# Attention by blocks of 256 queries, with one PSUM bank of value sums and two banks for the work placed in between

## The chip, the cores and the metric

The kernel runs on all 8 cores of one Trainium2 chip, each core on half of one of the four sequences. The time is device microseconds of the slowest core. The engines are called PE (TensorE matmul), PEld (its weight load), DVE (VectorE), ACT (ScalarE), POOL (GpSimd) and SP (SyncE).

## The reference, cut to what matters

```python
z = h @ w_in                                   # q, k, v, attention gate, pool input, pool gate
q, k: (B, S, 4 heads, 2, 64);  v: (B, S, 4 heads, 128)
# differential attention, causal, S = 4096
s = einsum('bqhcd,bkhcd->bhcqk', q, k) / 8     # c = 0, 1: two softmaxes of a head
a = softmax(where(causal, s, -inf))
a = a[:, :, 0] - lam * a[:, :, 1]
o = einsum('bhqk,bkhe->bqhe', a, v)
attn_out = rms_norm(o) * (1 - lam_init) * silu(g_attn)
pool_out = multiscale_pool(u) * silu(g_pool)
mix = concat(attn_out, pool_out) @ w_out
h = layer_norm(ALPHA * h + mix)
gate = sigmoid(h @ w_pg + b_pg)
out = h + (p @ w_pe) * gate
```

## The kernel before

Each core holds the keys and values of its whole sequence (8 slabs of 512 positions) and owns 4 groups j = 0 to 3 of 512 queries. All work is written into one stream for each engine in program order, with semaphores between them; an engine never reorders its stream.

The work has stages. Stage A projects the first slabs (no attention). Stage B holds the attention of j = 0 and 1, stage C that of j = 2, stage D that of j = 3. In each of B, C and D a list of other work ("filler") is laid between the pieces of attention: projections of later slabs in B and C; in D the output part, in tiles of 128 tokens: `q_M` (output projection, then the layer norm on DVE and POOL), `q_T` (transpose), `q_G` (gate projection) and `q_P` (embedding projection, product and store). Between the stages stand two blocks of pure projections, `block(5)` and `block(7)`. After D comes the tail, which finishes the tiles that are left.

Attention is a list of 160 steps. A step handles two blocks of 128 keys (u = 0, 1) against the 512 queries of one head. `qk(p)` makes the scores: for each u and softmax c one matmul of 64 rows, 128 keys and 512 queries, each into a PSUM bank of its own (banks 0 to 3); on the diagonal ("stair" steps, 4 for each j and head) the queries shrink to 512, 384, 256, 128 and four matmuls of 128 columns add the mask. ACT takes exp of each pair of banks into `PT[pi]` (L713). `lsum(p)` sums the columns of PT by four matmuls of 32 columns of ones, side by side in the four column tiles of the array, one for each (u, c), into bank 6. `av(p)` multiplies V with PT: four matmuls into banks 4 and 5, one bank for each softmax. The order in the stream is qk(p), lsum(p-1), filler, av(p-1), filler.

At the last step of a head DVE copies the sums to bf16 in two parts (`Lh`, then `Lhl`, L727 and L728) and the value sums to SBUF (`o12`, L744). Then two matmuls `q_sel` (L764) spread the row sums over the partitions, ACT takes Ln and Exp (L768, L770) for the reciprocal, DVE combines the two softmaxes (`fin_o`), squares and splits (`fin_sq`), two matmuls `q_ss` (L783) sum the squares, ACT makes the reciprocal root (L795, L797) and DVE multiplies into `mixT` (`mix`). `after(n, f)` puts f into the stream n calls of `tick()` later.

The filler is dealt out by `Feed`: `take(us)` issues matmuls of the current piece ("quantum", mostly 8 matmuls) until a budget is used or the quantum ends. The filler and the matmuls `q_sel` and `q_ss` all write one PSUM bank, `BF` = 7. So before q_sel or q_ss the quantum in progress is completed (`feed.finish()`), and its result must be read out of the bank (`evac`, L446, L507, L594, L649, L669, mostly on DVE).

```python
feed = Feed([BF])
...
if fq is not None:
    used = feed.take(budget)
    feed.finish()
...
if fq is not None:
    fq.mms[0](BF)
```

In the tail the last four tiles (12 to 15, the tokens of j = 3) go through M, T, G and P.

## Time and profile before

| what | value |
|---|---|
| runs | 829.9, 850.0 and 829.45 us, median 829.9 |
| profiled execution | 823.01 us, span 821.2 us |
| spans of the cores | 813.9 to 821.2 us |
| granted TensorE clock of the cores | 0.964 to 0.970 of full |
| busy of the span: PE, DVE, ACT, POOL | 85%, 45%, 50%, 16% |

The span is from the first to the last instruction of the slowest core; the profiled execution's own time has 1.8 us around it. The profile is that of this slowest core. It has the stages at these times: A 0 to 146.8 us, B to 309.8, block(5) to 325.6, C to 469.4, block(7) to 485.6, D to 743.5, tail to 821.2.

### The profile page before, as it was taken

How to read it: one execution, taken by the hardware profiler on the slowest of the kernel's cores; microseconds unless marked ns; L12 is line 12 of the kernel's file. 1: busy time of each engine (PE TensorE's matmuls, PEld its weight loads, DVE VectorE, ACT ScalarE, POOL GpSimd, SP SyncE). 2: the span in 40 equal slices, each digit the busy share in tenths (PEclk: the TensorE clock that was granted, in tenths of full speed). 3: DMA queues.
4: the chain of work that ended last, by engine and by line, in shares of the span. 5: the costliest groups of instructions: out<-in, count | busy, mean ns of one | idle time of the engine just before them, and what ended most of it. 6: DMA issues, size and time to landing. Idle time of an engine off the chain costs nothing.

```text
span 821.2 us, 9761 instructions; the slowest of 8 cores (813.9 to 821.2 us)
## 1 busy us (share of the span) xinstructions
PE 694.2 (85%) x4122; PEld 275.8 (34%) x4122; DVE 370.6 (45%) x544; ACT 414.3 (50%) x524; POOL 128.2 (16%) x101
## 2 busy tenths in 40 slices
PE   0899999877788989999998987988887987999473
PEld 0344444333233324333333332332332332334231
DVE  1124526354534572423225536444445555547922
ACT  0012112544556675667676644767653756654231
POOL 6000000000000000000000002333331332333322
PEclk9899999999999999999999999999998998999878
DMA  8997330303000000302334080011010141010012
GB/s 99 144 157 108 52 52 1 51 1 52 1 1 1 1 1 1 51 4 49 52 52 78 3 199 31 1 52 51 27 52 27 52 147 58 26 52 27 10 42 103
DMA packets 30187, 40.37 MB, mean 49 GB/s; under 512 B 6336, under 2 KB 25024, under 8 KB 30144
## 3 DMA queue, kind: packets, MB, share of 16 engines
q0 software_dynamic: 24240, 21.24, 18.8%
q1 hardware_dynamic: 5904, 18.52, 6.4%
q8 instruction: 32, 0.52, 0.3%
q14 instruction: 11, 0.09, 0.0%
HBM read 52.60 MB, written 8.39 MB: 74 GB/s over the span
## 4 chain that ended last, share of the span: by engine, by line
PE 60%; DVE 21%; ACT 10%; DMA 4%; issue 2%; POOL 2%; DVEq 0%; ACTq 0%; SPq 0%; POOLq 0%
PE psum_all L462 23%; PE psum_all L738 9%; PE psum_all L700 6%; PE psum_all L579 6%; PE psum_all L635 5%; ACT sb_PT L713 5%; PE psum_all L723 4%; DMA sb_wsec<-w_in 3%; PE psum_all L708 2%; DVE sb_st L597 2%; DVE sb_arena L649 2%; POOL sb_mv L602 1%; DVE sb_Lhl L728 1%; PE psum_all L764 1%; DVE sb_Lh L727 1%
## 5 line engine op out<-in xcount | busy, mean ns | idle before, releaser
L713 ACT ACTIVATE sb_PT<-psum_all 128x1024 bf16<-128x1024 f32 (+3 forms) x320 | 267.1, 891 | 99.2 <-PE psum_all L708 52.5
L462 PE MATMUL psum_all<-sb_xb,sb_wsec 128*128 128x512 bf16 x768 | 189.6, 387 | 19.3 <-DMA sb_wsec<-w_in 19.1
L738 PE MATMUL psum_all<-sb_PT,sb_Vt 128*128 128x512 bf16 (+3 forms) x640 | 146.5, 352 | 0.0
L462 PEld LDWEIGHTS psum_all<-sb_xb,sb_wsec 128*128 128x128 bf16 x768 | 72.1, 99 | 111.0 <-issue 30.6
L700 PE MATMUL psum_all<-sb_qT,sb_kT 64*128 64x512 bf16 (+3 forms) x640 | 94.0, 355 | 14.4 <-ACT sb_PT L713 10.6
L738 PEld LDWEIGHTS psum_all<-sb_PT,sb_Vt 128*128 128x128 bf16 x640 | 60.6, 99 | 61.5 <-issue 3.9
L462 PE MATMUL psum_all<-sb_wsec,sb_xb 128*128 128x512 bf16 x256 | 67.0, 397 | 3.9 <-DMA sb_wsec<-w_in 3.8
L579 PE MATMUL psum_all<-sb_wsec,sb_mixT 128*128 128x512 bf16 x256 | 64.4, 383 | 2.6 <-DVE sb_arena L623 1.8
L723 PE MATMUL psum_all<-sb_PT,sb_ones_bf 128*32 128x512 bf16 (+3 forms) x640 | 59.4, 361 | 0.0
L635 PE MATMUL psum_all<-sb_wsec,sb_arena 128*128 128x512 bf16 x192 | 50.6, 391 | 9.6 <-DVE sb_arena L649 9.4
L154 POOL DMA_DIRECT2D sb_xb<-xT x8 | 7.4, 919 | 307.2 <-PE psum_all L540 140.2
L700 PEld LDWEIGHTS psum_all<-sb_qT,sb_kT 64*128 64x128 bf16 x640 | 21.2, 94 | 82.8 <-ACT sb_PT L713 37.6
L446 DVE CAST sb_Vt<-psum_all 128x512 bf16<-128x512 f32 x22 | 15.1, 688 | 60.4 <-PE psum_all L462 60.4
L653 POOL TENSOR_SCALAR sb_arena<-sb_arena 128x1024 f32<-128x1024 f32 x11 | 31.1, 2832 | 55.9 <-ACT sb_arena L652 55.9
L764 PE MATMUL psum_all<-sb_Lhl,sb_sel 128*128 128x512 bf16 x32 | 12.7, 402 | 28.5 <-DVE sb_Vt L446 7.8
L462 PEld LDWEIGHTS psum_all<-sb_wsec,sb_xb 128*128 128x128 bf16 x256 | 23.7, 101 | 36.2 <-issue 8.3
L446 DVE CAST sb_kT<-psum_all 128x512 bf16<-128x512 f32 x22 | 15.1, 688 | 44.6 <-PE psum_all L462 44.6
L579 PEld LDWEIGHTS psum_all<-sb_wsec,sb_mixT 128*128 128x128 bf16 x256 | 22.4, 98 | 35.1 <-DVE sb_arena L623 6.0
L723 PEld LDWEIGHTS psum_all<-sb_PT,sb_ones_bf 128*32 128x32 bf16 x640 | 16.4, 92 | 45.2 <-issue 38.8
L649 DVE TENSOR_TENSOR sb_arena<-psum_all,sb_wsec 128x512 f32<-128x512 f32 x22 | 15.1, 687 | 36.0 <-PE psum_all L635 36.0
L669 DVE TENSOR_TENSOR sb_arena<-psum_all,sb_arena 128x512 f32<-128x512 f32 x28 | 19.2, 687 | 26.8 <-PE psum_all L663 26.7
L519 DVE TENSOR_TENSOR sb_arena<-sb_arena 128x572 f32<-128x572 f32 (+3 forms) x40 | 29.6, 741 | 1.4
(138 smaller groups left out, 694.9 us busy)
## 6 DMA issues: line engine op xcount, KB each, us to landing
sb_xb<-xT POOLq DMA_DIRECT2D x8, 1024.0 KB, 12.0
sb_wsec<-w_in POOLq DMA_DIRECT2D x5, 1024.0 KB, 45.3
sb_xb<-x_own SPq DMA_DIRECT2D x6, 512.0 KB, 4.9
out<-sb_xb SPq DMA_DIRECT2D x6, 512.0 KB, 2.7
sb_wsec<-w_out POOLq DMA_DIRECT2D x2, 1024.0 KB, 10.4
sb_wsec<-w_pg POOLq DMA_DIRECT2D x2, 1024.0 KB, 11.2
sb_kT<-x_own SPq DMA_DIRECT2D x4, 512.0 KB, 8.4
sb_xh<-x_own SPq DMA_DIRECT2D x3, 512.0 KB, 3.2
```

What stands on the lines that cost most here:

```text
L446: P.op(DVE, lambda e: e.tensor_copy(out=out_ap, in_=src), reads=[B_bank[bank]], writes=wbufs)
L462: P.op(PE, lambda e: e.matmul(ps[:, bank, :], a, b, start=(kc == 0), stop=(kc == 7)), reads=[bw, bx], writes=[B_bank[bank]], sig=(kc == 7))
L519: e.tensor_tensor(out=o, in0=a, in1=b, op=ALU.add), reads=[bs], writes=[bd])
L579: P.op(PE, lambda e: e.matmul(ps[:, bank, :], mixT[:, kc, tsl(t)], wo[nh][:, kc, :], start=(i == 0), stop=(i == 7)), reads=[B_w[1 + nh], B ...
L635: P.op(PE, lambda e: e.matmul(ps[:, bank, :], hb[hs(t)][:, kc * 128:(kc + 1) * 128], wg[nh][:, kc, :], start=(kc == 0 and t < 11), stop=(k ...
L649: P.op(DVE, lambda e: e.tensor_tensor(out=z[:, nh, :], in0=ps[:, bank, :], in1=bpgb[:, nh, :], op=ALU.add), reads=[B_bank[bank], bz], writ ...
L653: P.op(POOL, lambda e: e.tensor_scalar(out=z[:], in0=z[:], scalar1=2.0 ** 62, scalar2=None, op0=ALU.min), reads=[bz], writes=[bz])
L700: P.op(PE, lambda e, c=c, u=u, key0=key0: e.matmul(ps[:, 2 * u + c, q0:512], kT[64 * c:64 * c + 64, h, key0:key0 + 128], qT[j][64 * c:64 * ...
L713: P.op(ACT, lambda e, u=u, pi=pi: e.activation(out=PT[pi][:, :, q0:512], in_=ps[:, 2 * u:2 * u + 2, q0:512], func=AF.Exp), reads=[B_bank[2 ...
L723: P.op(PE, lambda e, c=c, r0=r0, pi=pi: e.matmul(ps[r0:r0 + 32, BL, q0:512], ones_bf[:, 0:32], PT[pi][:, c, q0:512], start=it["first"], st ...
L738: P.op(PE, lambda e, c=c, u=u, pi=pi, s=s, kb=kb: e.matmul(ps[:, BO + c, q0:512], Vt[:, s * 4 + kb, h * 128:(h + 1) * 128], PT[pi][:, c, q ...
L764: P.op(PE, lambda e: e.matmul(ps[:, bank, :], sel[:, c, :], Lhl[:], start=True, stop=True), reads=[B_Lhl, B_sel], writes=[B_bank[bank]])
```

## The change

- The queries are taken by 256. A group is (j, half hf, head h), 32 groups in place of 16. A unit is a pair of key blocks (k = 0, 1) against 256 queries; a step has two units. The scores of softmax c for both key blocks share one bank (2u + c), 256 columns each. There are 144 steps: 2j + 1 in the first half and 2j + 2 in the second, for each head. Only the last step of a group is masked; its units have 256 and 128 queries, and eight mask matmuls.
- Groups of j = 0 and j = 1 alternate in stage B. Stage B has 40 steps, C 44, D 60.
- `PT` is ordered key block, softmax, query, so a moving operand holds both softmaxes (512 columns). `lsum` has a column tile for each (u, key block), bank 5. `av` accumulates both softmaxes side by side in one bank, 4. In the first step of the groups of j = 0, hf = 0, a matmul with zeros opens the narrower column tiles.
- Banks 6 and 7 are both for filler; the matmuls q_sel and q_ss are issued by `Feed.now` into the other bank than that of the quantum in progress, which stays open.
- A group needs one `q_sel` matmul (before: two for a head) and two `q_ss` matmuls of 256 columns. Squaring moves from DVE to ACT, the split squares have buffers of their own (`sqx`), and there are six sets of finishing buffers, not two. Read-outs of filler by `evac` within attention are all on DVE.
- In stage D the first 256 queries of j = 3 are finished for all heads after 28 of 60 steps. The filler of D covers tiles 0 to 13 (M) in place of 0 to 11, G to tile 11, P to tile 10, T to tile 12, and T(0) comes after M(1). The tail finishes tiles 14 and 15, with T(14) and T(15) behind P(12) and P(13).

The diff, cut to its core (of what is removed, most stands in the functions above and is left out here; of the buffers, loads and hooks only the size of PT):

```diff
+    def _next(self):
+        b = self.banks[self.bi % len(self.banks)]
+        self.bi += 1
+        return b
+
     def _open(self):
         if self.cur is None and self.q:
             self.cur, self.k = self.q.popleft(), 0
-            self.bank = self.banks[self.bi % len(self.banks)]
+            self.bank = self._next()
+        return self.cur is not None
+
+    def now(self, q):
+        b = self._next()
+        if self.cur is not None:
             self.bi += 1
-        return self.cur is not None
+        for m in q.mms:
+            m(b)
+        q.end(b)
...
+        BL, BO = 5, 4
...
+        PT = [sb(f"PT{i}", [128, 2, 2, 256], BF16) for i in range(4)]
...
+                    if t + 4 < 14:
                         load_x(t + 4)
             return Quantum([mm(kc) for kc in range(2)], end, 2 * MM)
 
 
+        order = []
+        for hf in range(2):
+            for h in range(4):
+                order += [(0, hf, h), (1, hf, h)]
+        order += [(j, hf, h) for j in (2, 3) for hf in range(2) for h in range(4)]
         steps = []
...
+        for n_, (j, hf, h) in enumerate(order):
+            units = [((s, kb), (s, kb + 1), 0, False) for s in range(2 * j) for kb in (0, 2)]
+            units += [((2 * j, kb), (2 * j + 1, kb), 0, False) for kb in range(2 * hf)]
+            units += [((2 * j, 2 * hf + i), (2 * j + 1, 2 * hf + i), 128 * i, True) for i in range(2)]
+            for i in range(0, len(units), 2):
+                steps.append(dict(j=j, hf=hf, h=h, n=n_, slot=(n_ % 4 if j < 2 else 4 + n_ % 2), u=units[i:i + 2],
+                                  first=(i == 0), last=(i + 2 == len(units))))
         NS = len(steps)
...
         def qk(p):
             it = steps[p]
...
+            j, h, hf = it["j"], it["h"], it["hf"]
+            for u, (a, b, q0, msk) in enumerate(it["u"]):
+                for k, (s, kb) in enumerate((a, b)):
+                    key0 = s * GT + kb * 128
                     for c in range(2):
...
+                        P.op(PE, lambda e, c=c, u=u, k=k, key0=key0, q0=q0, msk=msk: e.matmul(
+                            ps[:, 2 * u + c, 256 * k + q0:256 * k + 256], kT[64 * c:64 * c + 64, h, key0:key0 + 128],
+                            qT[j][64 * c:64 * c + 64, h, 256 * hf + q0:256 * hf + 256], start=(k == 0), stop=(k == 1 and not msk)),
+                            reads=[B_k[h][s], B_q[h][j]], writes=[B_bank[2 * u + c]], sig=(c == 1 and k == 1 and not msk))
+            for u, (a, b, q0, msk) in enumerate(it["u"]):
+                if not msk:
+                    continue
+                for k, (s, kb) in enumerate((a, b)):
+                    mk = 2 if k else kb % 2
+                    for c in range(2):
+                        P.op(PE, lambda e, c=c, u=u, k=k, mk=mk, q0=q0: e.matmul(
+                            ps[:, 2 * u + c, 256 * k + q0:256 * k + q0 + 128], ident[:], tri3[:, mk, :], start=False, stop=(k == 1)),
+                            writes=[B_bank[2 * u + c]], sig=(c == 1 and k == 1), deps=t_id)
+            for u, (a, b, q0, msk) in enumerate(it["u"]):
                 pi = 2 * (p % 2) + u
...
+                P.op(ACT, lambda e, u=u, pi=pi, q0=q0: e.activation(
+                    out=PT[pi][:, :, :, q0:256].rearrange("p k c n -> p c k n"),
+                    in_=ps[:, 2 * u:2 * u + 2, :].rearrange("p c (k n) -> p c k n", k=2)[:, :, :, q0:256], func=AF.Exp),
+                    reads=[B_bank[2 * u], B_bank[2 * u + 1]], writes=[B_PT[pi]])
...
         def lsum(p):
             it = steps[p]
...
+            for u, (a, b, q0, msk) in enumerate(it["u"]):
                 pi = 2 * (p % 2) + u
...
+                for k in range(2):
+                    r0 = 32 * (2 * u + k)
+                    wide = it["first"] and q0 > 0
+                    if wide:
+                        P.op(PE, lambda e, k=k, r0=r0: e.matmul(ps[r0:r0 + 32, BL, :], zero[:], PT[2 * (p % 2)][:, k, :, :],
+                                                               start=True, stop=False),
+                             reads=[B_PT[2 * (p % 2)], B_one], writes=[B_bank[BL]], sig=False)
+                    P.op(PE, lambda e, k=k, r0=r0, pi=pi, q0=q0, wide=wide: e.matmul(
+                        ps[r0:r0 + 32, BL, :].rearrange("p (c n) -> p c n", c=2)[:, :, q0:256], ones_bf[:, 0:32], PT[pi][:, k, :, q0:256],
...
         def av(p):
             it = steps[p]
...
+            h = it["h"]
+            for u, (a, b, q0, msk) in enumerate(it["u"]):
                 pi = 2 * (p % 2) + u
...
+                for k, (s, kb) in enumerate((a, b)):
+                    P.op(PE, lambda e, k=k, u=u, pi=pi, s=s, kb=kb, q0=q0: e.matmul(
+                        ps[:, BO, :].rearrange("p (c n) -> p c n", c=2)[:, :, q0:256], Vt[:, s * 4 + kb, h * 128:(h + 1) * 128],
+                        PT[pi][:, k, :, q0:256], start=(it["first"] and u == 0 and k == 0), stop=(it["last"] and u == 1 and k == 1)),
+                        reads=[B_PT[pi], B_v[s * 4 + kb]], writes=[B_bank[BO]], sig=(k == 1))
             if it["last"]:
...
+        def q_sel(it):
+            f_ = it["slot"]
+            o_, r_, x_, bo, br, bx = o12[f_], rr[f_], sqx[f_], B_o12[f_], B_rr[f_], B_sqx[f_]
 
             def fin_o():
...
+                P.op(DVE, lambda e: e.tensor_tensor(out=o_[:], in0=o_[:], in1=r_[:], op=ALU.mult), reads=[bo, br], writes=[bo])
+                P.op(DVE, lambda e: e.scalar_tensor_tensor(out=o_[:, 0, :], in0=o_[:, 1, :], scalar=neglam, in1=o_[:, 0, :],
+                                                           op0=ALU.mult, op1=ALU.add), reads=[bo, B_sc], writes=[bo])
+                P.op(ACT, lambda e: e.activation(out=r_[:, 0, :], in_=o_[:, 0, :], func=AF.Square), reads=[bo], writes=[br])
+
+            def fin_sq():
+                P.op(DVE, lambda e: e.tensor_copy(out=x_[:, 0, :], in_=r_[:, 0, :]), reads=[br], writes=[bx])
+                P.op(DVE, lambda e: e.tensor_tensor(out=x_[:, 1, :], in0=r_[:, 0, :], in1=x_[:, 0, :], op=ALU.subtract),
+                     reads=[br, bx], writes=[bx])
+
+            def mm(bank):
+                P.op(PE, lambda e: e.matmul(ps[:, bank, :], sel[:, 1, :], Lhl[:], start=True, stop=True),
+                     reads=[B_Lhl, B_sel], writes=[B_bank[bank]])
+
+            def end(bank):
+                P.op(ACT, lambda e: e.activation(out=r_[:], in_=ps[:, bank, :].rearrange("p (c n) -> p c n", c=2), func=AF.Ln),
+                     reads=[B_bank[bank], bx], writes=[br])
+                P.op(ACT, lambda e: e.activation(out=r_[:], in_=r_[:], func=AF.Exp, scale=-1.0), reads=[br], writes=[br])
+                after(2, fin_o)
+                after(4, fin_sq)
+            return Quantum([mm], end, MM)
...
+            def mm(i):
+                def f(bank):
+                    P.op(PE, lambda e: e.matmul(ps[:, bank, 0:256], ones_bf[:], x_[:, i, :], start=(i == 0), stop=(i == 1)),
+                         reads=[bx, B_one], writes=[B_bank[bank]], sig=(i == 1))
+                return f
+
+            def mix():
                 P.op(DVE, lambda e: e.tensor_tensor(out=o_[:, 0, :], in0=o_[:, 0, :], in1=r_[:, 0, :], op=ALU.mult),
...
+                     reads=[bo, br], writes=[bo])
                 P.op(DVE, lambda e: e.scalar_tensor_tensor(out=mixT[:, h, tok], in0=o_[:, 0, :], scalar=gsc, in1=mixT[:, h, tok],
                                                            op0=ALU.mult, op1=ALU.mult),
                      reads=[bo, B_sc, B_mix[h][j]], writes=[B_mix[h][j]])
 
```

The filler of stage D, the loop and the tail:

```diff
         fillC += [hook(k7[0], lambda: wload(pTb[:], pT_d.rearrange("(kc p) t -> p kc t", p=128), [B_xb[0]]))] + k7[1:]
         fillC += v7[:3] + [hook(v7[3], load_wout)] + q_q(7) + q_halo(7) + u7[:3] + [hook(u7[3], load_wpg)]
         fillD = []
-        for k in range(12):
+        for k in range(14):
             fillD += [q_M(k, 0), q_M(k, 1)]
-            if k >= 1 and k < 11:
+            if k == 1:
+                fillD += [q_T(0)]
+            if 1 <= k < 13:
                 fillD += [q_G(k - 1, 0), q_G(k - 1, 1)]
-            if k >= 2:
+            if 2 <= k < 13:
                 fillD += [q_P(k - 2, 0), q_P(k - 2, 1)]
-            if k < 11:
+            if 1 <= k < 13:
                 fillD += [q_T(k)]
...
+            budget = feed.left() * weight(p) / sum(weight(i) for i in range(p, end_p))
             tick()
...
+            used = feed.take(budget / 2)
             if p > 0:
                 av(p - 1)
                 if steps[p - 1]["last"]:
...
+                    fins.setdefault(p, []).append(q_sel(steps[p - 1]))
+                    fins.setdefault(p + 3, []).append(q_ss(steps[p - 1]))
             tick()
...
+            for q in fins.pop(p, []):
+                feed.now(q)
+            feed.take(budget - used)
...
+        last = steps[NS - 1]
+        M = {(t, nh): q_M(t, nh) for t in range(14, 16) for nh in range(2)}
+        emit(M[14, 0], 0, 0, 7)
+        emit(M[14, 1], 1, 0, 7)
+        emit(q_sel(last), 6)
+        for p in sorted(fins):
+            for q in fins[p]:
+                emit(q, 7)
+        emit(q_G(12, 0), 5)
+        emit(q_G(12, 1), 6)
+        tail[0] = True
+        emit(q_T(13), 7)
+        emit(M[15, 0], 2, 0, 7)
+        emit(M[15, 1], 3, 0, 7)
         tick()
+        emit(q_P(11, 0), 5)
+        emit(q_P(11, 1), 6)
+        emit(q_ss(last), 7)
         tick()
         tick()
+        emit(q_G(13, 0), 4)
+        emit(q_G(13, 1), 5)
+        for t in (14, 15):
             for nh in range(2):
+                emit(M[t, nh], 2 * (t - 14) + nh, 7)
+        fe = Feed([6, 7, 4, 5, 0, 1, 2, 3])
+        fe.q.extend([q_P(12, 0), q_P(12, 1), q_P(13, 0), q_P(13, 1), q_T(14), q_T(15), q_G(14, 0), q_G(14, 1), q_G(15, 0), q_G(15, 1),
+                     q_P(14, 0), q_P(14, 1), q_P(15, 0), q_P(15, 1)])
```

## Rows read from the trace of the kernel before

**Rows 1.** The page: busy us, share of the span and instructions of each engine

```profile
PE 694.2 (85%) x4122; PEld 275.8 (34%) x4122; DVE 370.6 (45%) x544; ACT 414.3 (50%) x524; POOL 128.2 (16%) x101
```

**Rows 2.** Busy time by stage: us, PE, PEld, DVE, ACT, POOL (xinstructions), clock, DMA share, GB/s

```profile
146.80:309.80 163.00, 136.23 (x933) 53.95 (x933) 82.00 (x120) 95.70 (x132) 0.88 (x1) 0.97 0.09 13
325.60:469.40 143.80, 134.40 (x881) 49.77 (x882) 53.93 (x81) 98.01 (x123) 4.38 (x6) 1.00 0.25 41
485.60:743.50 257.90, 221.93 (x1336) 81.67 (x1337) 134.62 (x179) 157.63 (x182) 80.35 (x54) 0.97 0.15 54
743.50:784.50 41.00, 25.43 (x131) 11.60 (x128) 33.59 (x47) 15.16 (x17) 16.89 (x13) 0.85 0.07 26
784.50:821.20 36.70, 23.11 (x111) 10.15 (x111) 8.43 (x10) 7.63 (x12) 8.01 (x4) 0.83 0.18 72
```

**Rows 3.** Groups of TensorE instructions: shape, count, busy us, mean ns, idle before, releaser

```profile
L635 PE MATMUL psum_all<-sb_wsec,sb_arena 128*128 128x512 bf16 x192 | 50.6, 391 | 9.6 <-DVE sb_arena L649 9.4 <-DVE sb_xh L594 0.2
...
L663 PE MATMUL psum_all<-sb_wsec,sb_xb 128*128 128x512 bf16 x64 | 18.5, 390 | 8.5 <-DVE sb_arena L669 8.1 <-ACT sb_qT L768 0.3
...
L764 PE MATMUL psum_all<-sb_Lhl,sb_sel 128*128 128x512 bf16 x32 | 12.7, 402 | 28.5 <-DVE sb_Vt L446 7.8 <-DVE sb_kT L446 5.2 <-DVE sb_arena L500 4.6
...
L783 PE MATMUL psum_all<-sb_Lh,sb_ones_bf 128*128 128x512 bf16 x16 | 6.2, 388 | 5.6 <-DVE sb_kT L446 2.8 <-DVE sb_Vt L446 1.8 <-DVE sb_arena L649 0.9
```

**Rows 4.** Longest wait of TensorE for exp: us in total, times, longest

```profile
PE psum_all L700 <- ACT sb_PT L713: 10.6, 27, 0.9
```

**Rows 5.** Timeline of TensorE in two diagonal steps: start us, us, instruction

```profile
153.61 0.39 PE L700 MATMUL psum_all<-sb_qT,sb_kT 64*128 64x256 bf16 x4
153.93 0.40 PE L708 MATMUL psum_all<-sb_tri,sb_ident 128*128 128x128 bf16 x4
...
157.69 0.60 PE L700 MATMUL psum_all<-sb_qT,sb_kT 64*128 64x512 bf16 x4
158.22 0.40 PE L708 MATMUL psum_all<-sb_tri,sb_ident 128*128 128x128 bf16 x4
158.55 0.24 PE L723 MATMUL psum_all<-sb_PT,sb_ones_bf 128*32 128x128 bf16 x4
```

**Rows 6.** Timeline of TensorE: a step without filler, then projection matmuls

```profile
299.69 0.40 PE L723 MATMUL psum_all<-sb_PT,sb_ones_bf 128*32 128x512 bf16 x4
300.02 1.04 PE L738 MATMUL psum_all<-sb_PT,sb_Vt 128*128 128x512 bf16 x4
300.99 0.61 PE L700 MATMUL psum_all<-sb_qT,sb_kT 64*128 64x512 bf16 x4
...
309.81 10.52 PE L462 MATMUL psum_all<-sb_xb,sb_wsec 128*128 128x512 bf16 x48
```

**Rows 7.** Timeline of all engines around the end of a head in stage B

```profile
173.40 0.24 PE L723 MATMUL psum_all<-sb_PT,sb_ones_bf 128*32 128x128 bf16 x4
...
174.41 0.75 DVE L728 SCALAR_TENSOR_TENSOR sb_Lhl<-sb_Lh,sb_hl,psum_all 128x512 bf16<-128x512 bf16 x1
```

**Rows 8.** Groups of ScalarE instructions by shape

```profile
L713 ACT ACTIVATE sb_PT<-psum_all 128x1024 bf16<-128x1024 f32 x224 | 215.2, 1019 | 61.5 <-PE psum_all L700 46.1 <-PE psum_all L708 15.0
...
L768 ACT ACTIVATE sb_qT<-psum_all 128x512 f32<-128x512 f32 x18 | 10.6, 595 | 31.6 <-PE psum_all L764 31.6
```

**Rows 9.** Timeline of all engines after the last step of attention

```profile
743.29 0.40 PE L738 MATMUL psum_all<-sb_PT,sb_Vt 128*128 128x128 bf16 x4
...
753.48 3.24 POOL L653 TENSOR_SCALAR sb_arena<-sb_arena 128x1024 f32<-128x1024 f32 x1 [6.35 <-ACT sb_arena L652]
...
758.68 0.69 DVE L594 SCALAR_TENSOR_TENSOR sb_kT<-sb_kT,psum_all 128x512 f32<-128x512 f32 x1 [1.24 <-PE psum_all L579]
...
771.07 1.06 ACT L587 ACTIVATE sb_PT<-sb_kT 128x1024 bf16<-128x1024 f32 x1 [4.37 <-DVE sb_kT L584]
...
784.56 3.59 PE L635 MATMUL psum_all<-sb_wsec,sb_PT 128*128 128x512 bf16 x8 [12.47 <-ACT sb_PT L621]
```

**Rows 10.** Timeline of the last matmuls

```profile
807.81 1.89 PE L663 MATMUL psum_all<-sb_wsec,sb_xb 128*128 128x512 bf16 x8
```

More of the change, by code:

```diff
@@ L566, in build_nc @@
         tail = [False]
+        made = set()
         def load_x(t):
@@ L695, in qk @@
             it = steps[p]
-            j, h, q0 = it["j"], it["h"], it["q0"]
-            for u, (s, kb) in enumerate(it["u"]):
-                key0 = s * GT + kb * 128
-                for c in range(2):
-                    P.op(PE, lambda e, c=c, u=u, key0=key0: e.matmul(
-                        ps[:, 2 * u + c, q0:512], kT[64 * c:64 * c + 64, h, key0:key0 + 128],
-                        qT[j][64 * c:64 * c + 64, h, q0:512], start=True, stop=(not it["stair"])),
-                        reads=[B_k[h][s], B_q[h][j]], writes=[B_bank[2 * u + c]], sig=(c == 1 and not it["stair"]))
@@ L733, in av @@
             it = steps[p]
-            q0, h = it["q0"], it["h"]
-            for u, (s, kb) in enumerate(it["u"]):
+            h = it["h"]
+            for u, (a, b, q0, msk) in enumerate(it["u"]):
                 pi = 2 * (p % 2) + u
-                for c in range(2):
-                    P.op(PE, lambda e, c=c, u=u, pi=pi, s=s, kb=kb: e.matmul(
-                        ps[:, BO + c, q0:512], Vt[:, s * 4 + kb, h * 128:(h + 1) * 128], PT[pi][:, c, q0:512],
-                        start=(it["first"] and u == 0), stop=(it["last"] and u == 1)),
-                        reads=[B_PT[pi], B_v[s * 4 + kb]], writes=[B_bank[BO + c]], sig=(c == 1))
@@ L763, in mm @@
+                P.op(DVE, lambda e: e.tensor_tensor(out=x_[:, 1, :], in0=r_[:, 0, :], in1=x_[:, 0, :], op=ALU.subtract),
+                     reads=[br, bx], writes=[bx])
             def mm(bank):
-                P.op(PE, lambda e: e.matmul(ps[:, bank, :], sel[:, c, :], Lhl[:], start=True, stop=True),
+                P.op(PE, lambda e: e.matmul(ps[:, bank, :], sel[:, 1, :], Lhl[:], start=True, stop=True),
                      reads=[B_Lhl, B_sel], writes=[B_bank[bank]])
             def end(bank):
-                P.op(ACT, lambda e: e.activation(out=r_[:, c, :], in_=ps[:, bank, :], func=AF.Ln), reads=[B_bank[bank]], writes=[br[c]])
@@ L924, in build_nc @@
                 lsum(p - 1)
-            wsum = sum(weight(i) for i in range(p, end_p))
-            budget = feed.left() * weight(p) / wsum
-            fq = fins.pop(p, None)
-            eng[0] = 0
+            budget = feed.left() * weight(p) / sum(weight(i) for i in range(p, end_p))
             tick()
-            if fq is not None:
-                used = feed.take(budget)
-                feed.finish()
-            else:
-                used = feed.take(budget / 2)
+            used = feed.take(budget / 2)
             if p > 0:
```

220 lines of the change are left out of this document (82 added, 138 removed).

## The prediction

> **What bounds the kernel now.** I read the engines' shares first: TensorE is busy 694.2 of 821.2 us, 85%, DVE 45% and ACT 50% [rows 1]. Then the stages. In B, C and D TensorE is busy for 136.2 of 163.0, 134.4 of 143.8 and 221.9 of 257.9 us: it is the bound there, and stands still for 26.8, 9.4 and 36.0 us, 72 together. The tail is another matter: 77.7 us with 48.5 us of TensorE work, and in its first 41 us DVE is busy for 33.6 [rows 2]. So there are three places to look: the work of TensorE in attention, its 72 us of waits, and a tail that DVE bounds.
>
> The waits have a clear owner. L764 (q_sel) sat idle for 28.5 us before its matmuls, L783 (q_ss) for 5.6, the gate and embedding projections L635 and L663 for 9.6 and 8.5, nearly all released by a DVE instruction that reads bank 7 (L446, L500, L649, L669) [rows 3]: 52 us. With the smaller rows of the same kind (L579, 2.6 us, and a transpose that waits for its input, 4 us) I count 59. Waits of the scores for exp are only 10.6 us [rows 4].
>
> **The change part by part.**
>
> *Attention on TensorE.* I need the price of a run of matmuls. From start to start, four score matmuls of 512 columns, run in pairs, take 158.22 - 157.69 = 0.53 us, of 256 columns 0.32 us; four masks of 128 columns one after the other 0.33 us [rows 5]. Four row sums, side by side, take 0.33 us, four value sums 0.97 us [rows 6]. A matmul of 512 columns in a long run takes 10.4/48 = 0.216 us [rows 6]. All fit one form: 0.11 us to enter a run, and columns at 0.216 us for 512 (half for pairs, a quarter for the row sums). The total of columns is unchanged. So a full step costs 0.53 + 0.33 + 0.97 = 1.83 us in both kernels, though it now has eight score matmuls of 256 columns. Before: 96 full steps, 176 us, and 16 diagonals of four steps. One diagonal costs 1.50 (scores) + 1.32 (masks) + 1.00 + 2.59 = 6.41 us, together 103: 278. After: 112 full steps, 205 us, and 32 masked ones at 0.43 + 0.54 + 0.33 + 0.75 = 2.05 us, 66: 271. The finishing matmuls go from 16 x 1.19 us to 32 x 0.65, +2. I take -5 us. The price of the third and fourth pair in a run is not in the trace: nothing if the next weights are loaded behind a running pair, and 0.09 us each (the spacing that four masks show, 0.33/4 = 0.08, is as near) if they are not. The constant of 0.11 us is the same in the row sums, which never reload behind a running matmul, so a reload inside a run of scores seems hidden; I take nothing and keep up to +27 us (two more changes of pair, 144 steps, 0.094 us).
>
> On this point the Trainium skill speaks against the change (TensorE: Matmul & The Clock Gate, "The mechanism"): a weight load overlaps a running matmul only where their row groups differ. The third pair uses the row groups of the first. By that rule the sum would be some 27 us worse. The run of four at 256 columns shows no such cost, but has one change of pair only.
>
> *The single bank.* With two banks in turn, q_sel and q_ss no longer wait until the last filler is read out, and a quantum no longer waits for the one before it. The 59 us go. What is late next: q_sel needs Lhl. Row sums started at 173.40 and Lhl ended at 174.41 + 0.75 = 175.16, 1.76 us later, on a free DVE [rows 7]. In the new B and C the budget is about 1 us of filler in a step; between the start of the row sums and q_sel lie 0.33 + 0.11 + 0.5 + 0.97 = 1.9 us. So the wait is nothing if DVE is free and all of DVE's backlog if not. Bounds for one wait: 0 and 2.8 us (the longest wait of L764 now, released by a read-out). DVE will be busy for about 70% in B and 60% in D, so I take 0.7 us, 32 times: 22 us. Behind q_sel on TensorE are the rest of the filler and the next scores. For what is left of read-out and POOL waits in D I keep 6 us. Net -31 us.
>
> *ACT and DVE.* Exp loses 32 instructions' fixed part: 1.02 us for 1024 columns [rows 8], so -5 us in all. A group's Ln, Exp, Square, Ln, Exp is about 2.45 us, 32 times, against 3.6 us, 16 times: +21. ACT goes from 96 to some 114 us in B, of about 155; DVE gains some 25 us there. Both stay under TensorE, but ACT now has 2.9 us of work in a step of B against 3.2 on TensorE. The wait for exp, 10.6 us [rows 4], I raise by 3 (bounds 0 and +15). The cover is that scores of step p+1 need only exp of step p, which stands ahead of Ln and Exp in ACT's stream. One value bank in place of two must be copied out before the next group's av; between them lie a q_sel, filler, scores and row sums, over 3 us against a copy of 0.7: nothing. Row sums are as well covered.
>
> *Clock.* B and D have 0.97 of the clock [rows 2]; with half the waits I give back 3 us.
>
> *Stage D gets work from the tail.* Tiles 12 and 13 of M, two G, one P and two T are 68 matmuls of 0.216 us and 16 of 0.062: +16 us. T(0) is one quantum later, its 4 us are in the 59.
>
> *The tail.* Now: the last value sums end at 743.7, the first M of the tail is read at 758.68, the second tile's cast starts at 771.07, and G(12) starts only at 784.56, because four tiles pass the layer norm on DVE first; the last matmul ends at 807.81 + 1.89 = 809.7, and 11.5 us of products, additions and store follow [rows 9, 10]. After: two tiles only. The first read-out is about 3 us later, since gate2(12) now stands on ACT ahead of the last group's Ln, and it waits for a POOL instruction of 3.24 us that ended 13 us after the last value sums [rows 9]. The second tile is cast at 772.1 (+3), then T(15) and its read-out 1.6 us; T(15) stands ahead of G(14), so G starts at 772.7 (+3). G(14) and G(15) are 36 matmuls: 11 at half clock (3.59 us for 8, less the last one's own length, as at 784.56 [rows 9]) and 25 at full, 10.1 us; P 1.8 us. End of TensorE 784.6 (+3) in place of 809.7, and the same 11.5 us behind. So -22 us (bounds -15 and -27).
>
> **Sum.** -5 - 31 + 3 - 3 + 16 - 22 = -42 us of 823.0 in the profiled execution: 781. The median of the runs shown is 829.9, 0.8% above that, so in its terms -42 us and the same share: 829.9 x 781/823 = 787 us. A measurement of this kernel tells about 2%, 17 us, from no change.
>
> **The rivals.** (1) *The reload of the weights shows.* Two more pair changes in each step at 0.094 us: 787 + 27 = 814 us. For it: doubling the score matmuls halves the time that hides a load. Against: the 0.32 us for 256 columns [rows 5]. (2) *The waits move and don't shrink:* q_sel waits for Lhl, and ACT's added 16 us for exp; the 72 us stay. Then the sum is -5 + 16 - 22 = -11: 819 us. For it: DVE and ACT both get more to do in B. Against: six sets of buffers and one step more of slack for each piece. (3) *Slower than before: DVE's backlog ahead of Lhl.* DVE takes its stream in order, and Lh and Lhl now stand 32 times behind whatever was put there before, a pool chain or a layer norm with its wait for POOL. At 2.8 us for each group the waits cost 32 x 2.1 = 67 us more than I took: 787 + 67 = 854 us. It decides from 0.7 + 43/32 = 2.0 us in the mean. Against: today's longest waits, 2.8 us, are the rare ones. (4) *Better:* q_sel hardly waits and the clock holds: 787 - 22 = 765 us.
>
> On entering runs, the Trainium skill (TensorEngine Tiling (Array Packing), "Key Properties") says that a change of tiling mode drains the array; the 0.11 us at each entry agree, and fewer steps mean fewer of them, which is in the -5.
>
> **How the numbers follow.** Forecast 0.60 (around 787, from 772 to 802), rival 1 0.09, rival 2 0.12, rival 3 0.05, rival 4 0.14. The range of 8 in 10: 762 to 814, which leaves out most of rival 2 and rival 3 and the far end of rival 4. Faster by over 2% (under 813) holds the forecast, rival 4 and half of rival 1: 0.80. Within 2%: 0.14. Slower: 0.06.
>
> **What would show it.** Score runs of eight matmuls at 0.53 us start to start (rival 1: 0.6 to 0.75). L764 idle some 22 us, with Lhl as releaser, not L446 or L649 (rival 3: over 60). L635 and L663 idle near nothing inside D. ACT in B near 114 us, the wait for exp under 20 us. B near 155, C near 141, D near 248 us, the tail near 55 us with G(14) some 32 us after the last value sums. Wrong would make me: a queue on DVE in B that I can't see from averages, stage D not taking 16 us of work without new waits, or the last group's finishing chain in the tail longer than 17 us.

## The result

The changed kernel takes 756.9 us (756.35 to 757.95, 4 runs) against 829.7 us: ratio 0.913, 95% interval 0.911 to 0.915. The forecast was 787 us with a range of 762 to 814: right in sign, 30 us short, and the time lies 5 us below the range. Some executions of every kernel are slowed because a part of the cores gets a lower clock (850.0 us here); ratios, and the medians of the experiments below, leave them out. The profiled execution shown here has 756.4 us and a span of 754.9. Against the profiled 823.0 us of the kernel before, in whose terms the forecast's sum was made, it is 66.6 us faster where the sum had 42, so 25 us of the 30 are the sum's. The other 6 come from the step to the median: the profiled execution before was 6.7 us quicker than its median, that of the changed kernel 0.5.

The page of the changed kernel, busy us and share of the span, and below it the windows of its stages B with block(5), C with block(7), D, and the tail in two parts (the columns as in [rows 2]):

```profile
PE 662.3 (88%) x4458; PEld 295.9 (39%) x4542; DVE 407.5 (54%) x666; ACT 428.9 (57%) x564; POOL 135.4 (18%) x105
```

```profile
147.00:308.16 161.16, 142.66 (x1070) 64.00 (x1090) 97.95 (x182) 110.84 (x164) 0.88 (x1) 0.98 0.09 13
308.16:459.03 150.87, 143.33 (x1065) 63.52 (x1085) 68.58 (x120) 107.68 (x140) 5.81 (x7) 1.00 0.32 51
459.03:697.10 238.07, 220.76 (x1576) 97.58 (x1606) 159.55 (x226) 167.24 (x199) 92.50 (x62) 1.00 0.18 62
697.10:731.90 34.80, 23.21 (x119) 11.13 (x120) 26.26 (x38) 13.28 (x17) 14.17 (x11) 0.91 0.08 31
731.90:754.90 23.00, 11.32 (x46) 4.72 (x44) 5.70 (x6) 3.47 (x6) 5.73 (x3) 0.72 0.24 92
```

From first scores to first scores, stage B with its block takes 161.2 us (before: 178.8), C 150.9 (160.0), D 238.1 (257.9), the tail 57.8 (77.7) [rows 2]. So 17.6, 9.1, 19.8 and 19.9 us. With the blocks of 15.8 and 16.2 us added, the forecast's stages were 170.8, 157.2 and 248 us and the tail 55: B, C and D are each 6 to 10 us better than forecast, the tail 3 us worse. The granted clock of D is 1.00, not 0.97, with more work in it; the tail's second part has 0.72.

What TensorE waits for (us in total, times, longest):

```profile
PE psum_all L733 <- ACT sb_PT L748: 10.5, 16, 1.6
PE psum_all L805 <- DVE sb_Lhl L770: 10.3, 26, 2.0
...
PE psum_all L482 <- issue: 3.8, 22, 0.3
...
PE psum_all L659 <- DVE sb_arena L647: 1.5, 1, 1.5
...
PE psum_all L805 <- DVE sb_kT L466: 0.8, 1, 0.8
```

L805 is q_sel, L733 the scores, L659 the gate projection, L482 a projection of a later slab. The 59 us of stops for read-outs [rows 3] are down to a few, and Lhl is late next, as forecast, but with 10.3 us, not 22. The wait for exp is 10.5 us, as before [rows 4]. All waits of TensorE in B, C and D sum to 75 us before and to 41 us now, and 7 of these 41 are gaps with no releaser ("issue"): this trace lacks some matmul records (736 of 768 in the largest group), the run without finishing lacks none and has no such gaps. So the waits fell by 41 us, to 34.

Steps in D (start, duration; read the differences of the starts):

```profile
467.37 0.61 PE L733 MATMUL psum_all<-sb_qT,sb_kT 64*128 64x256 bf16 x8
467.91 0.40 PE L764 MATMUL psum_all<-sb_PT,sb_ones_bf 128*32 128x512 bf16 x4
468.24 1.25 PE L601 MATMUL psum_all<-sb_wsec,sb_mixT 128*128 128x512 bf16 x5
469.33 1.03 PE L780 MATMUL psum_all<-sb_PT,sb_Vt 128*128 128x512 bf16 x4
470.20 0.81 PE L601 MATMUL psum_all<-sb_wsec,sb_mixT 128*128 128x512 bf16 x3
470.94 0.61 PE L733 MATMUL psum_all<-sb_qT,sb_kT 64*128 64x256 bf16 x8
471.48 0.40 PE L764 MATMUL psum_all<-sb_PT,sb_ones_bf 128*32 128x512 bf16 x4
471.81 1.25 PE L601 MATMUL psum_all<-sb_wsec,sb_mixT 128*128 128x512 bf16 x4
472.90 1.03 PE L780 MATMUL psum_all<-sb_PT,sb_Vt 128*128 128x512 bf16 x4
473.77 0.38 PE L824 MATMUL psum_all<-sb_qT,sb_ones_bf 128*128 128x256 bf16 x2
473.99 0.81 PE L601 MATMUL psum_all<-sb_wsec,sb_mixT 128*128 128x512 bf16 x3
```

Eight score matmuls of 256 columns take 467.91 - 467.37 = 0.54 us, as the form forecast [rows 5]: a second change of pair costs nothing. At 473.77 the two q_ss matmuls (L824) run in the other bank, 0.22 us, in the middle of an output-projection quantum (L601: five matmuls ahead of av by the spacing, of which the trace holds four, and three behind), and nothing waits.

The tail: last value sums, first M that needs them, the casts of tiles 14 and 15, T(15), G(14), last matmuls:

```profile
696.25 0.82 PE L780 MATMUL psum_all<-sb_PT,sb_Vt 128*128 128x512 bf16 x4
...
717.87 1.04 PE L601 MATMUL psum_all<-sb_wsec,sb_mixT 128*128 128x512 bf16 x4 [0.22 <-DVE sb_mixT L831]
...
725.29 1.06 ACT L610 ACTIVATE sb_PT<-sb_kT 128x1024 bf16<-128x1024 f32 x1 [5.95 <-DVE sb_kT L607]
...
729.99 1.06 ACT L610 ACTIVATE sb_PT<-sb_kT 128x1024 bf16<-128x1024 f32 x1 [3.65 <-DVE sb_kT L607]
...
731.10 1.03 PE L637 MATMUL psum_all<-sb_ident,sb_PT 128*128 128x128 bf16 x8 [3.67 <-ACT sb_PT L610]
...
732.36 2.77 PE L659 MATMUL psum_all<-sb_wsec,sb_PT 128*128 128x512 bf16 x6
...
741.55 1.89 PE L689 MATMUL psum_all<-sb_wsec,sb_xb 128*128 128x512 bf16 x8
```

The last value sums end at 697.1; T(15) is 34.0 us later and G(14) starts at once after it, where four tiles let G(12) start only after 40.9 us [rows 9]. The forecast had G(14) after 32 us.

### The profile page after: what moved, and what is told of

Same layout as the page of the kernel before. It is cut to its first block, busy times and chain, and to the rows that moved or that the text cites. A ratio compares the mean times of both kernels' runs of the same rounds, so it can differ in the third digit from the quotient of the medians.

```text
span 754.9 us, 10683 instructions; the slowest of 8 cores (749.6 to 754.9 us)
## 1 busy us (share of the span) xinstructions
PE 662.3 (88%) x4458; PEld 295.9 (39%) x4542; DVE 407.5 (54%) x666; ACT 428.9 (57%) x564; POOL 135.4 (18%) x105
## 4 chain that ended last, share of the span: by engine, by line
PE 69%; DVE 16%; ACT 6%; DMA 4%; issue 3%; POOL 1%; another core or an unknown queue 0%; DVEq 0%; SPq 0%; POOLq 0%
PE psum_all L482 26%; PE psum_all L780 11%; PE psum_all L733 8%; PE psum_all L601 7%; PE psum_all L659 6%; PE psum_all L764 5%; DMA sb_wsec<-w_in 3%; ACT sb_PT L748 3%; DVE sb_Lhl L770 2%; DVE sb_Lh L769 2%; PE psum_all L743 2%; ACT sb_arena L678 1%; DVE sb_arena L675 1%; DVE sb_arena L539 1%; PE psum_all L805 1%
## 5 line engine op out<-in xcount | busy, mean ns | idle before, releaser
L748 ACT ACTIVATE sb_PT<-psum_all 128x1024 bf16<-128x1024 f32 (+1 forms) x288 | 263.9, 970 | 70.6 <-PE psum_all L733 45.6
L482 PE MATMUL psum_all<-sb_xb,sb_wsec 128*128 128x512 bf16 x736 | 183.1, 383 | 26.0 <-DMA sb_wsec<-w_in 20.7
L780 PE MATMUL psum_all<-sb_PT,sb_Vt 128*128 128x512 bf16 (+1 forms) x565 | 140.5, 369 | 2.9 <-issue 1.3
L482 PEld LDWEIGHTS psum_all<-sb_xb,sb_wsec 128*128 128x128 bf16 x768 | 71.2, 98 | 112.4 <-issue 35.6
L733 PE MATMUL psum_all<-sb_qT,sb_kT 64*128 64x256 bf16 (+1 forms) x1152 | 89.1, 266 | 13.9 <-ACT sb_PT L748 10.5
L733 PEld LDWEIGHTS psum_all<-sb_qT,sb_kT 64*128 64x128 bf16 x1152 | 43.4, 94 | 82.6 <-issue 33.7
L482 PE MATMUL psum_all<-sb_wsec,sb_xb 128*128 128x512 bf16 x242 | 64.0, 388 | 7.8 <-DMA sb_wsec<-w_in 4.3
L601 PE MATMUL psum_all<-sb_wsec,sb_mixT 128*128 128x512 bf16 x247 | 60.8, 380 | 2.5 <-DVE sb_mixT L831 1.0
L764 PE MATMUL psum_all<-sb_PT,sb_ones_bf 128*32 128x512 bf16 (+1 forms) x576 | 58.3, 381 | 0.0
L659 PE MATMUL psum_all<-sb_wsec,sb_arena 128*128 128x512 bf16 x213 | 54.0, 380 | 2.9 <-DVE sb_arena L647 1.5
L769 DVE CAST sb_Lh<-psum_all 128x512 bf16<-128x512 f32 x32 | 22.1, 690 | 46.0 <-PE psum_all L764 46.0
L466 DVE CAST sb_Vt<-psum_all 128x512 bf16<-128x512 f32 x24 | 16.6, 690 | 50.9 <-PE psum_all L482 49.2
L679 POOL TENSOR_SCALAR sb_arena<-sb_arena 128x1024 f32<-128x1024 f32 x13 | 36.1, 2775 | 39.5 <-ACT sb_arena L678 39.5
L466 DVE CAST sb_kT<-psum_all 128x512 bf16<-128x512 f32 x23 | 15.9, 690 | 41.1 <-PE psum_all L482 41.0
L482 PEld LDWEIGHTS psum_all<-sb_wsec,sb_xb 128*128 128x128 bf16 x256 | 23.3, 99 | 36.8 <-issue 8.0
L601 PEld LDWEIGHTS psum_all<-sb_wsec,sb_mixT 128*128 128x128 bf16 x256 | 23.7, 98 | 32.0 <-issue 2.9
L659 PEld LDWEIGHTS psum_all<-sb_wsec,sb_arena 128*128 128x128 bf16 x224 | 20.3, 98 | 28.4 <-issue 3.4
L506 ACT ACTIVATE sb_PT<-psum_all 128x512 f32<-128x512 f32 x16 | 9.6, 598 | 38.0 <-PE psum_all L482 31.9
## 6 DMA issues: line engine op xcount, KB each, us to landing
sb_wsec<-w_pg POOLq DMA_DIRECT2D x2, 1024.0 KB, 10.8
```

What stands on the lines that cost most here:

```text
L466: P.op(DVE, lambda e: e.tensor_copy(out=out_ap, in_=src), reads=[B_bank[bank]], writes=wbufs)
L482: P.op(PE, lambda e: e.matmul(ps[:, bank, :], a, b, start=(kc == 0), stop=(kc == 7)), reads=[bw, bx], writes=[B_bank[bank]], sig=(kc == 7))
L601: P.op(PE, lambda e: e.matmul(ps[:, bank, :], mixT[:, kc, tsl(t)], wo[nh][:, kc, :], start=(i == 0), stop=(i == 7)), reads=[B_w[1 + nh], B ...
L659: P.op(PE, lambda e: e.matmul(ps[:, bank, :], hb[hs(t)][:, kc * 128:(kc + 1) * 128], wg[nh][:, kc, :], start=(kc == 0 and t < 13), stop=(k ...
L679: P.op(POOL, lambda e: e.tensor_scalar(out=z[:], in0=z[:], scalar1=2.0 ** 62, scalar2=None, op0=ALU.min), reads=[bz], writes=[bz])
L733: P.op(PE, lambda e, c=c, u=u, k=k, key0=key0, q0=q0, msk=msk: e.matmul(ps[:, 2 * u + c, 256 * k + q0:256 * k + 256], kT[64 * c:64 * c + 6 ...
```

## The experiments

Each is timed against the kernel before on the same chip. Beside them the kernel before had medians of 828 to 829 us, with single runs from 823 to 833, so an absolute time compares across chips to some 3 us.

**One bank for filler and finishing.**

```diff
-        feed = Feed([6, 7])
+        feed = Feed([7])
...
             for q in fins.pop(p, []):
+                feed.finish()
                 feed.now(q)
```

> The changed kernel with one bank for the filler and for the matmuls q_sel and q_ss: the quantum in progress is completed before q_sel and q_ss, as in the kernel before. Everything else stays: 256 queries, 144 steps, the tail. Theory A (the two banks carry the gain inside the attention, through the waits and through the clock that the waits cost): the waits of L805, L824, L659 and L689 come back, 33 us or more in sum, the granted clock in stage D falls below 0.98, and the time is 757 + 30 to 45 = 787 to 802 us. Theory B (the gain came from fewer steps, fewer mask runs and fewer entries of runs, and from slack between the pieces): 757 + 10 to 20 us = under 777 us.

Measured: 884 us, ratio 1.065 (1.061 to 1.069): 127 us more than the changed kernel and 54 more than the kernel before. Its stages B, C and D, and one stop in B:

```profile
147.20:364.90 217.70, 168.75 (x1090) 67.22 (x1089) 98.76 (x182) 112.48 (x164) 0.87 (x1) 0.87 0.06 9
364.90:539.40 174.50, 151.62 (x1086) 62.48 (x1085) 68.25 (x120) 108.48 (x140) 5.80 (x7) 0.99 0.28 46
539.40:823.97 284.57, 238.18 (x1606) 97.22 (x1606) 161.91 (x226) 168.47 (x199) 94.90 (x62) 0.96 0.15 51
```

```profile
202.08 0.68 DVE L466 CAST sb_kT<-psum_all 128x512 bf16<-128x512 f32 x1
...
202.82 0.61 PE L805 MATMUL psum_all<-sb_Lhl,sb_sel 128*128 128x512 bf16 x1 [2.72 <-DVE sb_kT L466]
...
203.47 0.60 ACT L809 ACTIVATE sb_Vt<-psum_all 128x512 f32<-128x512 f32 x1 [0.85 <-PE psum_all L805]
...
204.12 1.03 PE L482 MATMUL psum_all<-sb_xb,sb_wsec 128*128 128x512 bf16 x2 [0.69 <-ACT sb_Vt L809]
```

A DVE read-out (L466) ends, q_sel runs, ACT takes Ln (L809), and only then may filler go on: two stops in a step, the first 2.7 us long. In B the clock is 0.87. Both theories were too small. With filler on both sides of av the second bank is a condition, not an addition; with the old loop it is not, as two runs below show.

**The groups of j = 3 by head, four tiles in the tail.**

```diff
+        order += [(2, hf, h) for hf in range(2) for h in range(4)]
+        order += [(3, hf, h) for h in range(4) for hf in range(2)]
...
-        for k in range(14):
+        for k in range(12):
```

> The changed kernel with the groups of j = 3 in the order head, half (not half, head): tiles 12 to 15 all need the last head, so the filler of stage D ends at tile 11 as before and the tail finishes four tiles in the order of the kernel before. Two banks and 256 queries stay. Theory A: the tail's DVE chain returns, the tail is 18 to 24 us longer, and stage D gives back the work of TensorE that left it, 14 to 17 us: net +3 to +9, 760 to 766 us. Theory B: stage D doesn't shrink by that work, since it has other limits, and the whole tail comes on top: 757 + 20 = 777 us. Theory C: the tail was worth nothing because the clock and the waits in D get better without the added tiles: 750 to 757 us.

Measured: 773.4 us, +16.5, ratio to the kernel before 0.934. Stage D and the tail:

```profile
457.50:686.00 228.50, 211.68 (x1526) 91.01 (x1526) 133.95 (x203) 162.46 (x194) 78.17 (x52) 0.99 0.17 58
686.00:770.30 84.30, 51.14 (x250) 22.55 (x247) 44.41 (x61) 21.76 (x28) 26.49 (x18) 0.85 0.15 57
```

D gives back 9.6 us for some 16 of work, the tail grows by 26.5, from 57.8 to 84.3, which is 6.6 more than the tail of the kernel before. So most of the tail's gain is net; the time lies between theories A and B.

**q_sel and q_ss behind the step's filler.**

```diff
             for q in fins.pop(p, []):
                 feed.now(q)
-            feed.take(budget - used)
```

(and take stands ahead of the loop.)

> The changed kernel with q_sel and q_ss issued after the second half of a step's filler, not ahead of it. Theory A (q_sel waits only for Lhl on DVE, 10.3 us in 26 waits): these waits fall under 3 us and the time to 757 - 5 to 9 = 748 to 752 us. Theory B (the wait is slack that moves to the next scores, which then wait for exp behind a later Ln and Exp on ACT): the wait of the scores for exp grows from 10.5 to 17 us or more, and the time stays at 755 to 759 us.

Measured: 754.5 us, ratio 0.910 (0.909 to 0.912), the lowest of the kernels that compute all, though the interval touches that of the changed kernel. The wait for Lhl is gone from the list, and the scores wait for exp 15.4 us:

```profile
PE psum_all L733 <- ACT sb_PT L748: 15.4, 22, 1.8
...
PE psum_all L805 <- DVE sb_kT L466: 2.2, 2, 1.8
```

The time lies at the edge of theory B (755 to 759) and the wait for exp grew by 5 us, not by the 6.5 or more of B: most of the 10 us are slack that moves, and some 2 us are gained.

**No finishing, changed kernel.** In the loop the two `fins` lines, in the tail q_sel and q_ss are taken out.

> The changed kernel without the finishing of a head: q_sel, q_ss and all that hangs on them (Ln, Exp, both softmaxes' combination, the rms norm and the product into mixT) are left out; the copies Lh, Lhl and o12 stay. It bounds what finishing costs after the change: 21 us of matmuls and entries on TensorE, 12.8 us of waits ahead of q_sel, some waits for exp. Theory A: 757 - 34 to 45 = 712 to 723 us, with some 10 us of that from the tail, where the last head's chain vanishes. Theory B (the finishing is mostly covered): above 730 us.

Measured: 716.8 us, -40. Theory A.

**No finishing, kernel before.** The same cut there.

> The kernel before without the finishing of a head: q_sel, q_ss and what hangs on them are left out, the copies Lh, Lhl and o12 stay. In the changed kernel the same cut was worth 40 us (716.8). Before, 19 us of matmuls and 34 us of waits stand ahead of or in q_sel and q_ss, and the low clock behind them. Theory A (the stops for the finishing were the old kernel's main loss, more than the 34 us its rows show): 830 - 65 to 85 = 745 to 765 us, with the granted clock at 0.98. Theory B (only the rows): 830 - 53 = 777 us.

Measured: 753.8 us, ratio 0.911 (0.907 to 0.916): -76 us by the medians, -74 by the ratio, as much as the whole change gained (-73). Theory A. Stages B, C and D, their blocks included:

```profile
144.40:290.10 145.70, 135.22 (x958) 55.88 (x976) 44.60 (x63) 82.69 (x112) 1.75 (x2) 1.00 0.09 13
290.10:437.40 147.30, 141.76 (x915) 53.61 (x934) 38.03 (x54) 92.83 (x113) 4.93 (x6) 1.00 0.33 56
437.40:672.00 234.60, 210.01 (x1296) 79.40 (x1322) 111.05 (x148) 144.71 (x162) 79.76 (x54) 0.99 0.16 58
```

The rows of q_sel and q_ss accounted for 53 us: 19 of matmuls, 34 of idle time. Between the two profiled executions the cut is worth 70 us (823.0 and 753.2), nearly all of it in B, C and D. TensorE's waits there fell from 75 to 36 us (without gaps that have no releaser), which is 5 more than the rows of q_sel and q_ss. Its busy time fell by 30 us, 11 more than their matmuls. The clock in B and D goes from 0.97 [rows 2] to 1.00 and 0.99: B and D had 10.8 + 15.5 us at half clock (twice the missing share, times the length), now 4.7, and that is up to 11 us of work. By this count little is left over. One thing this run doesn't separate: DVE and ACT lose work too (DVE 371 to 280 us, ACT 414 to 366), so filler is read out sooner. The longest wait of a gate projection for its read-out (L635 for L649) fell from 4.5 to 1.0 us, though no finishing matmul stands there.

**One bank with the old loop.**

```diff
-            used = feed.take(budget / 2)
+            if p in fins:
+                used = feed.take(budget)
+                feed.finish()
+            else:
+                used = feed.take(budget / 2)
...
+                    feed.finish()
...
+            if not fq:
+                feed.take(budget - used)
```

> The changed kernel with one bank for filler and finishing, and with the loop of the kernel before around them: in a step with a finishing matmul the whole budget of filler goes ahead of av, the quantum is completed, and nothing follows in the step. (The last filler is drained with a tick for each quantum.) The first version with one bank (884.6) had filler behind q_sel too, which waited for ACT. Theory A (each of the 64 finishing pieces costs a stop for a read-out, so 32 groups can't do with one bank): above the 830 us of the kernel before, 835 to 865 us. Theory B (the 884.6 was the bad placing): 775 to 800 us.

Measured: 814 us (812.2 to 814.7), ratio 0.985 (0.977 to 0.992). Neither range. With 64 finishing pieces in place of 48 the kernel as a whole is not slower than before if nothing follows q_sel in its step. So 70 of the 127 us of the first run came with its loop: filler behind q_sel in the same bank is the reason I see in its trace, but the old loop also places the rest of the filler otherwise.

**Two banks with the old loop (the quantum closed).** As above with `Feed([6, 7])`.

> The same loop as in the run with one bank and the old loop, but with two banks in turn: the quantum is completed ahead of q_sel and q_ss, which then go into the other bank. Theory A (what counts is that the finishing matmul doesn't wait for a read-out; keeping the quantum open is a detail): 757 + 3 to 12 = 760 to 769 us. Theory B (the uneven placing of filler by whole quanta makes TensorE wait for exp): 775 us or more.

Measured: 776.0 us, ratio 0.938. 38 us under the same loop with one bank, 19 over the changed kernel. Theory B, in the number and in what TensorE waits for:

```profile
PE psum_all L733 <- ACT sb_PT L748: 26.0, 36, 4.4
```

**No finishing, one bank.** The fourth run with `Feed([7])`.

> The changed kernel without finishing and with one bank, so that only the turn of bank from one filler quantum to the next is left of the single bank. It stands against 716.8 us with two banks, and against the kernel before without finishing, which has the same single bank and no finishing: between those two lie only the 256 queries with their steps and masks, and the tiles moved from the tail. Theory A (quantum after quantum costs little, since a step seldom begins two): 720 to 728 us. Theory B (a third or more of the single bank's 128 us is here): above 755 us.

Measured: 747.4 us, +30.6 against two banks. Filler behind filler in one bank alone costs that: I had priced it at 18 us, the idle before L635 and L663. The time lies between theories A and B. And 747.4 stands only 6 us under the kernel before without finishing.

**Open, but uneven,** and **closed, but even**: the old loop without its two `finish()`, and the changed loop with one `feed.finish()` ahead of `feed.now(q)`, both with two banks.

> Two banks, the quantum stays open, but in a step with a finishing matmul the filler is placed as before: the whole budget ahead of av, none behind q_sel or q_ss (last filler drained with a tick for each quantum). Against 756.9 us (filler on both sides, quantum open) and 776.0 us (this placing, quantum closed). Theory A (the 19 us between them come from closing the quantum, which makes the fill-in lumpy and the steps of unequal length): 757 to 763 us. Theory B (they come from the placing): 771 to 778 us.

> The other half of the pair: two banks, filler on both sides of av, but the quantum in progress is completed before q_sel and q_ss. One line is added to the changed kernel, and it is the same kernel as the first one with one bank (884.6 us) with bank 6 added to it. Theory A (closing costs): 770 to 778 us. Theory B (placing costs): 757 to 763 us. Either way the difference to 884.6 us, over 100 us, is the second bank alone at this placing.

Measured: 759.9 and 783.1 us. Theory A's cause in both, though the second is 5 us above its range: closing costs 16 us at one placing and 26 at the other; the placing of filler costs 3 if the quantum stays open. In the first of the two the scores wait for exp 15.9 us, where closing made it 26.0:

```profile
PE psum_all L733 <- ACT sb_PT L748: 15.9, 26, 2.1
```

In the second, a step can end its quantum early, run q_sel in the other bank and then begin a new quantum while both banks are still being read out, so filler (L482) waits for a read-out again:

```profile
PE psum_all L482 <- DVE sb_kT L466: 6.4, 5, 2.5
PE psum_all L482 <- DVE sb_Vt L466: 5.4, 8, 2.5
PE psum_all L482 <- DVE sb_arena L527: 4.8, 5, 1.4
...
PE psum_all L482 <- DVE sb_qT L468: 3.8, 4, 1.5
```

Against the first run, which differs in bank 6 alone, it is 101 us faster.

**More filler ahead of av** (`budget * 0.7`).

> The changed kernel with 70% of a step's filler ahead of av in place of half, so that Lhl has more time before q_sel. q_sel's wait for Lhl, 10.3 us, should fall to under 6 us; the steps' length doesn't change. If these waits are real losses: 757 - 4 to 7 = 750 to 753 us. If they only stand in for the wait for exp, as in the run with q_sel behind the filler (754.6 us): 754 to 758 us.

Measured: 763.1 us, +6, worse than each theory. q_sel still waits 7.9 us for Lhl, and the scores wait longer for exp, since less lies between av and them:

```profile
PE psum_all L733 <- ACT sb_PT L748: 14.9, 21, 3.4
...
PE psum_all L805 <- DVE sb_Lhl L770: 7.9, 14, 2.4
```

**The 256 queries alone:** one bank, the old loop, j = 3 by head. What came with them stays: Square on ACT, six sets of finishing buffers, read-outs within attention on DVE, T(0) one quantum later.

> The 256 queries alone: one bank, the loop of the kernel before (as in the run of 814.2 us), and the groups of j = 3 by head, so that the tail has its four tiles again (as in the run of 773.4 us). Against the kernel before only the blocks of 256 queries are left, with 144 steps, the one bank of value sums, 32 finishing chains of half the width, and T(0) one quantum later. My forecast's terms for these were -5 us for attention on TensorE, and about +3 for ACT. Theory A (they add up with the other parts): 814 + 16 = 830 us, within 8 us of the kernel before. Theory B (the tail's part was larger with one bank): 840 us or more. Theory C (the 256 queries are a gain by themselves): 815 us or less.

Measured: 820.0 us, ratio 0.991 (0.986 to 0.996), some 8 us under the kernel before. Between theories A and C.

## Why the prediction was wrong

The steps from the kernel before. The first is the rewritten attention as a whole, the last the two edits of the loop together. The first two times have an uncertainty of 4 and 6 us, from the intervals of their ratios, so the step of -6 between them is not larger than its own uncertainty:

| kernel | us | ratio | step, us |
|---|---|---|---|
| before | 829.7 | 1 | |
| 256 queries alone | 820.0 | 0.991 | -10 (by the ratio -8) |
| and two of four tiles out of the tail | 813.8 | 0.985 | -6 |
| and two banks, quantum closed | 776.0 | 0.938 | -38 |
| and quantum open, filler on both sides | 756.9 | 0.913 | -19 |

**The step that failed** is the single bank: "The 59 us go", with Lhl and a rest coming back, "Net -31 us", and "I give back 3 us" for the clock. Together -34, measured -57 by the table. The mechanism was right and the size of two terms was not. The profiled executions show which. In B, C and D together the forecast was -20 us and the measured change is -46.6. Half of the missing 27 us is in the waits: they fell by 41 us, from 75 to 34, where I had -28 with the exp term, and 12 of these 13 us are the wait for Lhl, 22 us in the sum and 10.3 measured. The other half is busy time of TensorE: I had +8 us (-5 for attention, -3 for the clock, +16 for the tiles) and it is about -6. The clock is the part of this that the traces show: 26 us of B and D ran at half clock before, 6 after, up to 10 us of work where I took 3. The last 7 us stay open; the attention term, below, may hold some of them. I took the idle rows for the whole price of the stops, and had the warning in hand: 0.97 of the clock in B and D [rows 2]. Cutting the finishing out of the kernel before showed the same: 70 us for 53 in rows, 11 of the difference in busy time.

**Lhl behind DVE's queue:** 22 us forecast, 10.3 measured, the right wait in the right order of rank, half the size. I had put DVE at 70% busy in B and 60% in D; it is 61% and 67%. That the lower load in B is the reason is not shown. Two attempts to remove it gained 2 us and lost 6. Rival 3 (2.8 us each) didn't come: the longest is 2.0.

**Attention on TensorE and ACT's load,** -5 and +3: the 256 queries alone gave -8 to -10, with 4 us of uncertainty, and the 4 us of T(0) are in that step too. ACT's total grew by 15 us, as the +16 had it; the forecast's own figure for B, 96 to 114, did not fit that total, and B with its block got 8 us more. The reload of weights (rival 1) is refuted: 0.54 us for eight matmuls with three changes of pair, against 0.53 for four of 512 columns with one. By the Trainium skill (TensorE: Matmul & The Clock Gate, "The mechanism") a weight load overlaps a running matmul only where their row groups differ. The trace does not agree with that rule here.

**Entering a run:** the 0.11 us is not paid at every run, as the form had it. Between runs that use the whole array it isn't there: four value sums ahead of filler take 470.20 - 469.33 = 0.87 us above, their columns alone, and 0.97 ahead of scores [rows 6]; the two q_ss matmuls between value sums and filler take 0.22. So the finishing matmuls cost 0.43 us a group where they stand like that, not 0.65.

**The tail,** -22 and +16 in D: measured -19.9 there. Its first read-out comes 21 us after the last value sums, where I had 18. The step in one-bank kernels is -6, as the sum said, within its uncertainty. But in the changed kernel the same move is worth 16.5 us. D pays about the same for the tiles in both, 11 and 10 us, not 16; the tail gains 17 us with one bank and 26.5 with two. With one bank and the old loop more filler is left over when D ends (202 matmuls run in the tail, against 165 recorded in the changed kernel). The two terms depend on the loop; I had added them as if they did not.

**The open quantum** has no term in my sum: I saw in the second bank only that "q_sel and q_ss no longer wait until the last filler is read out", not that the accumulation in progress need not be ended first. It is worth 16 to 26 us by itself. With two banks but a closed quantum the time is 776 us, inside my range. At the old placing closing makes the filler lumpy, and the scores behind a finishing matmul run into exp (26.0 against 15.9 us); at the new one filler waits for read-outs.

**Rival 2** (waits move, 819 us) had a grain: this is what happens to the last 10 us, not to the 59.

## What to carry to other kernels

Price a stop of TensorE by what goes when it goes, not by its idle row: here the rows showed 53 us and the cut gave 70 in the profiled execution. Look for stretches of half clock behind the longest stops and add them to the price. Give inserted work a bank of its own and leave the accumulation in progress open: 16 to 26 us here, beside 38 for the second bank itself. Splitting the work into finer groups pays mostly through what it frees (here a bank and two tiles of the tail): alone it gave 8 us, and with filler behind q_sel in the one bank it lost 54 (884 us against 830).
